# Logits of the first 128 rows: three products of rounded high and low parts in place of one product of whole fp32 values

## The chip, the cores and the metric

The kernel runs on one core of a Trainium2 chip. The time is device microseconds of that core, the median of several executions; the profile is one further execution. Engines: TensorE (PE for matmuls, PEld for its weight loads), VectorE (DVE), ScalarE (ACT), GpSimd (POOL) and SyncE (SP, which starts the large DMAs).

## The reference

Two layers over 256 tokens of width 1024, fp32 throughout. In each layer the normalised input goes through one input projection, whose columns serve two groups of heads: group A, sparse attention with 8 heads, whose keys are chosen by an indexer, and group B, differential attention with 4 pairs of maps, that is 8 maps too.

```python
for i in range(DEPTH):
    h = _rmsnorm(x, pre_norm_g[i])
    z = h @ w_in[i]
    qa, ka, va, qi, ki, wi, ga, qb, kb, vb, gb = _split_in(z)
    # rotary embedding on q and k of both groups
    oa = _dsa_attention(qa, ka, va, qi, ki, wi, top_k)   # logits = q k^T / 8, masked, softmax, times v
    ob = _diff_attention(qb, kb, vb, lam, lam_init, subln_g[i])
    y = jnp.concatenate([oa * jax.nn.silu(ga), ob * jax.nn.silu(gb)], axis=-1) @ w_out[i]
    x = x + _rmsnorm(y, post_norm_g[i])
    gate = jax.nn.sigmoid(x @ w_ple_gate[i])
    e = (p[i] @ w_ple_proj[i]) * gate
    x = x + _rmsnorm(e, ple_norm_g[i])
```

The attention is causal by chunks of 64 tokens. So rows 0 to 127 (block b = 0) need the keys 0 to 127 alone, and rows 128 to 255 (b = 1) need all 256.

## The kernel before

**Projections.** Each weight matrix is cut into units of 2 x 128 rows by 512 columns. ScalarE rounds a unit to fp32r (`w_hi`, line 637), VectorE subtracts that from the original (`w_lo`, line 835), and TensorE forms each product from three matmuls: high by high, high by low, low by high (lines 1233 to 1235). The activations are split in the same way. One step `mm` is a unit on one block of rows: 2 x 3 = 6 matmuls of 512 columns.

**Order.** `layer_steps` writes one list of steps for a layer, and every engine walks this same list and picks out its own part of each step. The projection chunks KB, VB, QA, KA, VA, GB, GA have 8 `mm` steps each, numbered 0, 1, 2, ... through all of them. `PLACE` says behind which of these numbers an attention step stands: `T` (transposes of q or k), `S` (logits), `E` (exponentials), `R` (reciprocals and mixing), `PT` (transposes of probabilities), `PV` (product with v). Within one number a `T` comes before an `S`, and both before an `E` and the `topk` rounds. The work of an engine runs strictly in this order, and semaphores tie the engines together.

**Queries and keys.** A step `T` transposes 128 tokens of a chunk with four PE transposes into the one PSUM bank `tr`. The next user of `tr` on PE, another `T` or a `PT`, waits until `tr` has been read (`wait_tr`, semaphore `tr_out`, line 1122). Who reads it depends on the block and chunk:

- queries, b = 0: ScalarE copies them whole, fp32, into `qT[g]` (line 714), and that frees `tr`;
- queries, b = 1: ScalarE writes the rounded `q_hi` (line 716), then VectorE `q_lo` (line 930), and that frees `tr`;
- keys, both blocks: ScalarE writes `k_hi` (line 720), then VectorE `k_lo` (line 934), and that frees `tr`. For b = 0 ScalarE first makes a whole copy `kT` (line 719).

**Logits.** `S` 0 and `S` 3 are the logits of b = 0 for groups B and A; `S` 1, 2, 4 and 5 are those of b = 1. Eight maps lie as four pairs: the even map of a pair on partitions 0 to 63, the odd one on 64 to 127, with 64 values per head. For b = 0 each map is one fp32 matmul of 128 queries by 128 keys from `qT` and `kT` (line 1161); for b = 1 it is three fp32r matmuls of 128 queries by 256 keys (lines 1163 and 1164). All are issued at line 1166. VectorE then adds the mask and takes the maximum (line 986), ScalarE the exponential (line 732).

`S` of b = 0 waits on `qk_hi_done`, that is on ScalarE's `k_hi` of the same keys; `S` of b = 1 waits on `tr_out` of its keys, that is on VectorE's `k_lo`. `kT` serves a second time, as the place of the last transposed probabilities. `p_hi` and `p_lo` hold the split per-layer embedding; they are read at a layer's first four `mm` steps and written again towards the end of the layer.

Of the kernel before, what the change touches and what calls it, by code (L numbers as in the profile page):

```python
# [22 lines left out]
P = 128  # L23
NB = SEQ // P
KT = D_MODEL // P
HEAD = 64
# [32 lines left out]
for _i, _u in enumerate(UNITS):  # L59
# [17 lines left out]
    QB=[5, 3],  # L77
    KB=[9, 12],
    QA=[25, 29],
    KA=[32, 37],  # L80
    S=[12, 15, 18, 34, 42, 43],
    E=[13, 16, 24, 36, 42, 43],
    R=[16, 16, 19, 19, 24, 24, 40, 43, 44, 44, 44, 45],
    PT=[19, 23, 26, 40, 41, 45, 46, 50, 51],
# [132 lines left out]
def build(nc, x, p, pre_norm_g, w_in, w_out, post_norm_g, lambda_q1, lambda_k1, lambda_q2, lambda_k2, subln_g,  # L217
# [6 lines left out]
    with ctx:  # L224
# [16 lines left out]
        p_hi = sb("p_hi", [P, NB, D_PLE // P, P], f32r)  # L241
# [11 lines left out]
        q_hi = sb("q_hi", [P, 4, P], f32r)  # L253
        q_lo = sb("q_lo", [P, 4, P], f32r)

        y_mix = [[qT[g][:, :, b * P:(b + 1) * P] for b in range(NB)] for g in range(2)]
        e_g = [qT[b][:, :, :].rearrange("p j t -> p (j t)") for b in range(NB)]
        probs = sb("probs", [P, 4, N])
# [120 lines left out]
        tr_steps = [s for s in layer_steps(0) if s[0] in ("TI", "T", "PT")]  # L379
        TRN = len(tr_steps)  # L380

        QK_WHOLE = [("QB", 0), ("QA", 0)]
        QK_SPLIT = [s[1:] for s in tr_steps if s[0] == "T" and s[1:] not in QK_WHOLE]

        def tr_index(L, s):

            return L * TRN + tr_steps.index(s) + 1
# [206 lines left out]
        def _(act):  # L594
            def copy(dst, src, scale=1.0):
                return nc.scalar.activation(dst, src, ACT.Copy, scale=scale)  # L596
# [27 lines left out]
            for pos, (L, s) in enumerate(STEPS):  # L624
# [83 lines left out]
                elif kind == "T":  # L708
                    chunk, b = s[1:]
                    act.wait_ge(tr_done, tr_index(L, s))  # L710
                    g, src = int(chunk[1] == "A"), tr[:, :].rearrange("p (j t) -> p j t", j=4)

                    if chunk[0] == "Q" and b == 0:
                        copy(qT[g][:, :, 0:P], src, HEAD ** -0.5).then_inc(tr_out, 1)
                    elif chunk[0] == "Q":
                        copy(q_hi[:, :, :], src, HEAD ** -0.5).then_inc(qk_hi_done, 1)
                    else:
                        if b == 0:
                            copy(kT[:, :, :], src)
                        copy(k_hi[:, :, b * P:(b + 1) * P], src).then_inc(qk_hi_done, 1)  # L720
                elif kind == "D":
                    for i in range(4):
# [74 lines left out]
        def _(dve):  # L797
# [31 lines left out]
            for pos, (L, s) in enumerate(STEPS):  # L829
# [89 lines left out]
                elif kind == "ylo":  # L919
# [1 line left out]
                    dve.wait_ge(at_hi, L * 12 + t8_index("y", b, 0) + 1)  # L921
                    nc.vector.tensor_tensor(act_lo[:, b, 0:4, :], y_mix[1][b], act_hi[:, b, 0:4, :].bitcast(fp32),
                                            ALU.subtract).then_inc(at_lo, 1)
                elif kind == "T" and s[1:] not in QK_WHOLE:

                    chunk, b = s[1:]
                    src = tr[:, :].rearrange("p (j t) -> p j t", j=4)
                    dve.wait_ge(qk_hi_done, L * 6 + QK_SPLIT.index(s[1:]) + 1)
                    if chunk[0] == "Q":
                        ins = nc.vector.scalar_tensor_tensor(q_lo[:, :, :], src, HEAD ** -0.5,  # L930
                                                             q_hi[:, :, :].bitcast(fp32), ALU.mult,
                                                             ALU.subtract)
                    else:
                        ins = nc.vector.tensor_tensor(k_lo[:, :, b * P:(b + 1) * P], src,  # L934
                                                      k_hi[:, :, b * P:(b + 1) * P].bitcast(fp32), ALU.subtract)
# [156 lines left out]
        def _(pe):  # L1092
# [60 lines left out]
            def logits(L, n, g, b, keys):  # L1153

                for j in range(N // keys):
                    for part in range(1 if b == 0 else 3):
                        for odd in range(2):
                            m = s_task(2 * n + odd)[2][j]
                            rows = slice(odd * HEAD, (odd + 1) * HEAD)
                            if b == 0:  # L1160
                                q, k = qT[g][rows, m // 2, 0:P], kT[rows, m // 2, :]
                            else:
                                q = (q_lo if part == 2 else q_hi)[rows, m // 2, :]
                                k = (k_lo if part == 1 else k_hi)[rows, m // 2, :]
                            end = part == (0 if b == 0 else 2)
                            ins = nc.tensor.matmul(s_bank(2 * n + odd)[:, j * keys:(j + 1) * keys], q, k,  # L1166
                                                   start=(part == 0), stop=end)
                            if end and j == N // keys - 1:
                                ins.then_inc(s_done, 1)
# [16 lines left out]
            for pos, (L, s) in enumerate(STEPS):  # L1186
# [147 lines left out]
                elif kind == "D":  # L1334

                    pe.wait_ge(tr_out, tr_index(L, ("TI", 1)))
                    pe.wait_ge(at_lo, L * 12 + 4)
                    for b in range(NB):
                        keys = (b + 1) * P
                        for j in range(2):  # L1340
                            for odd in range(2):
                                rows = slice(odd * HEAD, (odd + 1) * HEAD)
                                ins = nc.tensor.matmul(dots_of(b, odd)[:, j * keys:(j + 1) * keys],
                                                       idxT[rows, j, b * P:(b + 1) * P], idxT[rows, 2, 0:keys],
                                                       start=True, stop=True)
                                if j == 1:
                                    ins.then_inc(dots_done, 1)
                elif kind == "S" and s[1] not in S_WITH.values():
                    g, b, _, keys = s_task(2 * s[1])
                    keys_from = ("KB" if g == 0 else "KA", b)  # L1350
                    if b == 0:
                        pe.wait_ge(qk_hi_done, L * 6 + QK_SPLIT.index(keys_from) + 1)
                    else:
                        pe.wait_ge(tr_out, tr_index(L, ("T",) + keys_from))
                    if s[1] == 0:
                        pe.wait_ge(relu_done, L * 4 + 4)
                    else:
                        pe.wait_ge(max_done, L * 12 + {1: 2, 3: 4, 4: 8}[s[1]])
                    logits(L, s[1], g, b, keys)
                    if s[1] == 1:  # L1360
                        pe.wait_ge(z_out, L * 8 + 2)
                        logits(L, 2, g, b, keys)
                    elif s[1] == 4:
                        pe.wait_ge(max_done, L * 12 + 6)
                        logits(L, 5, g, b, keys)
                elif kind == "PT":
                    n = s[1]
                    g, b, tiles = pt_task(n)
                    wait_tr(L, s)
                    if g == 0:  # L1370
                        pe.wait_ge(mix_done, L * 3 + n + 1)
                    else:
                        pe.wait_ge(exp_done, L * 12 + tiles[1][2] + 1)
                    for j, (h, kt, si, col) in enumerate(tiles):
                        last = nc.tensor.transpose(tr[:, j * P:(j + 1) * P], probs[:, si % 4, col:col + P],  # L1375
                                                   ident[:, :])
                    last.then_inc(tr_done, 1)
                elif kind == "PV":
                    m = s[1]
                    g, b, _ = pt_task(PV_TASKS[m][0])  # L1380
                    pe.wait_ge(v_out, L * 4 + 2 * g + b + 1)
                    if m == 0:
                        pe.wait_ge(p_lo_done, L + 1)
                    for gi, (_, _, members) in enumerate(PV_GROUP):
                        if gi and m == members[0]:
                            pe.wait_ge(pv_out, L * 4 + gi)
                    pe.wait_ge(tr_out, tr_index(L, ("PT", PV_TASKS[m][-1])))
                    for n, j, (h, kt, si, col) in [(n, j, tile) for n in PV_TASKS[m]
                                                   for j, tile in enumerate(pt_task(n)[2])]:
                        if g == 0:  # L1390
                            last = nc.tensor.matmul(pv[:, h * P:(h + 1) * P], pt_slot(n)[:, j, :],  # L1391
                                                    v_all[:, kt, 0, h * P:(h + 1) * P], start=(kt == 0),
                                                    stop=(kt == b))
                        else:
                            rows = slice(h % 2 * HEAD, (h % 2 + 1) * HEAD)
                            last = nc.tensor.matmul(pv[rows, h // 2 * P:(h // 2 + 1) * P],  # L1396
                                                    v_all[:, kt, 1, h * HEAD:(h + 1) * HEAD], pt_slot(n)[:, j, :],
                                                    start=(kt == 0), stop=(kt == b), skip_group_check=True)
                    last.then_inc(pv_done, 1)
# [30 lines left out]
```

## Time and profile before

| | us |
|---|---|
| median of 3 executions | 359.07 (358.68 to 359.42) |
| the profiled execution, its own time | 359.26 |
| its span, first to last instruction | 357.5 |
| PE busy | 350.0 |
| PEld busy | 291.9 |
| DVE busy | 264.5 |
| ACT busy | 228.6 |
| POOL busy | 67.2 |

The mean granted clock of TensorE is 0.997 of full speed. In the views, "idle before" is the time that an engine stood still ahead of an instruction, and the arrow names what ended it. Where like instructions follow each other, a row gives the start of the first, the time from there to the end of the last, and their number. An fp32 matmul appears as two MATMUL records, an fp32r matmul as one (the page prints f32 for both), as the counts show: 8 fp32 matmuls in an `S` of b = 0 are 16 records.

### The profile page before, as it was taken

What the parts mean: (1) busy time and instruction counts of PE and PEld (TensorE: products, weight loads), DVE (VectorE), ACT (ScalarE), POOL (GpSimd) and SP (SyncE); (2) the same over time, 40 slices, a digit from 0 to 9 for tenths busy, and PEclk for the clock granted to TensorE, in tenths of its full rate; (3) what the DMA queues carried; (4) which work ended last, traced back from release to release, by engine and by line L of the source; (5) the groups of instructions that cost most, each with busy time, mean ns of one, the idle gap of its engine ahead of it and who ended that gap; (6) DMA issues with size and microseconds to landing.
All of it is one profiled execution on the core that took longest, in us unless ns stands there. A gap on an engine that the chain in (4) does not pass through costs nothing.

```text
span 357.5 us, 5709 instructions
## 1 busy us (share of the span) xinstructions
PE 350.0 (98%) x1927; PEld 291.9 (82%) x1927; DVE 264.5 (74%) x562; ACT 228.6 (64%) x459; POOL 67.2 (19%) x121
## 2 busy tenths in 40 slices
PE   8999999999999999999999999999999999999992
PEld 7887888888888888888888888788888888888882
DVE  3886979988946766786797487988895668678543
ACT  4897557777678945555757665778658686365221
POOL 1076261142200000013106433014220000000000
PEclk9999999999999999999999999999999999999998
DMA  7996488762754454647575927556355446550011
GB/s 287 381 336 216 130 193 200 257 177 68 224 169 131 129 195 149 210 158 154 179 231 158 353 82 207 147 129 178 107 168 155 151 141 213 175 169 11 0 50 69
DMA packets 31820, 61.12 MB, mean 171 GB/s; under 512 B 2376, under 2 KB 4432, under 8 KB 31792
## 3 DMA queue, kind: packets, MB, share of 16 engines
q1 hardware_dynamic: 30656, 57.48, 50.5%
q0 software_dynamic: 1120, 3.28, 4.8%
q8 instruction: 16, 0.26, 0.3%
q14 instruction: 12, 0.10, 0.1%
q10 hardware_dynamic: 16, 0.00, 0.0%
HBM read 59.71 MB, written 1.05 MB: 170 GB/s over the span
## 4 chain that ended last, share of the span: by engine, by line
PE 96%; issue 2%; DVE 1%; ACT 0%; POOLq 0%; DVEq 0%; POOL 0%
PE proj L1233 26%; PE proj L1235 25%; PE proj L1234 25%; PE sc L1314 3%; PE tr L1375 2%; PE sc L1166 2%; PE tr L1332 2%; PE pv L1396 2%; PE pv L1391 1%; PE proj L1177 1%; PE proj L1150 1%; PE proj L1166 1%; PE proj L1246 1%; PE proj L1139 1%; PE sc L1184 1%
## 5 line engine op out<-in xcount | busy, mean ns | idle before, releaser
L1233 PE MATMUL proj<-w_hi,act_hi 128*128 128x512 f32 (+1 forms) x392 | 157.4, 402 | 0.0
L1235 PE MATMUL proj<-w_hi,act_lo 128*128 128x512 f32 (+1 forms) x392 | 152.2, 388 | 0.0
L1234 PE MATMUL proj<-w_lo,act_hi 128*128 128x512 f32 (+1 forms) x392 | 151.6, 387 | 0.0
L835 DVE TENSOR_TENSOR w_lo<-raw,w_hi 128x1024 fp32r<-128x1024 f32 (+1 forms) x102 | 121.6, 1210 | 11.1 <-ACT w_hi L596 10.5
L596 ACT ACTIVATE w_hi<-raw 128x1024 fp32r<-128x1024 f32 (+2 forms) x103 | 102.5, 1022 | 2.4 <-PE proj L1235 1.8
L1235 PEld LDWEIGHTS proj<-w_hi,act_lo 128*128 128x128 f32 x392 | 73.5, 188 | 15.5
L1233 PEld LDWEIGHTS proj<-w_hi,act_hi 128*128 128x128 f32 x392 | 73.7, 188 | 14.6 <-issue 1.0
L1234 PEld LDWEIGHTS proj<-w_lo,act_hi 128*128 128x128 f32 x392 | 73.8, 188 | 12.8
L537 POOL TENSOR_TENSOR rstd<-var,minus_half 128x1 f32<-128x1 f32 x12 | 7.6, 640 | 191.6 <-DVE var L823 162.7
L732 ACT ACTIVATE probs<-probs,neg_max 128x128 f32<-128x128 f32 (+1 forms) x64 | 28.2, 444 | 6.0 <-DVE neg_max L986 6.0
L527 POOL TENSOR_TENSOR v_all<-work,rot_tab 128x128 f32<-128x128 f32 x16 | 10.6, 664 | 77.6 <-ACT work L596 77.5
L596 ACT ACTIVATE act_hi<-sc 128x512 fp32r<-128x512 f32 x20 | 11.3, 598 | 17.6 <-PE sc L1314 16.0
L596 ACT ACTIVATE pT<-tr 128x512 f32<-128x512 f32 (+1 forms) x20 | 11.4, 572 | 10.2 <-PE tr L1375 6.9
L915 DVE TENSOR_TENSOR act_lo<-sc,act_hi 128x512 fp32r<-128x512 f32 x16 | 10.4, 684 | 5.9 <-ACT act_hi L596 5.9
L934 DVE TENSOR_TENSOR k_lo<-tr,k_hi 128x512 fp32r<-128x512 f32 x8 | 5.5, 688 | 10.5 <-ACT k_hi L596 10.5
L732 ACT ACTIVATION_READ_ACCUMULATOR probs<-probs,neg_max 128x1 f32 x64 | 12.1, 189 | 0.0
L961 DVE MAX8 top<-score 128x8 f32<-128x128 f32 (+1 forms) x32 | 11.5, 358 | 0.6
L1375 PEld LDWEIGHTS tr<-ident,probs 128*128 128x128 f32 x72 | 8.8, 140 | 2.7 <-ACT pT L596 0.7
L962 DVE MATCH_REPLACE8 score<-top,score 128x128 f32<-128x128 f32 (+1 forms) x32 | 11.0, 343 | 0.0
L1375 PE MATMUL tr<-ident,probs 128*128 128x128 f32 x72 | 10.9, 273 | 0.0
L1051 DVE TENSOR_TENSOR work<-work,emb 128x512 f32<-128x512 f32 x7 | 4.8, 687 | 7.2 <-ACT work L768 7.2
L528 POOL TENSOR_TENSOR v_all<-work,rot_tab 128x64 f32<-128x64 f32 x16 | 10.1, 632 | 0.0
(209 smaller groups left out, 441.1 us busy)
## 6 DMA issues: line engine op xcount, KB each, us to landing
raw<-in_w_in_dram SPq DMA_DIRECT2D x59, 512.0 KB, 4.2
raw<-in_w_out_dram SPq DMA_DIRECT2D x16, 512.0 KB, 3.4
raw<-in_w_ple_gate_dram SPq DMA_DIRECT2D x16, 512.0 KB, 3.7
raw<-in_w_in_dram SPq DMA_DIRECT2D x7, 324.0 KB, 5.0
raw<-in_w_ple_proj_dram SPq DMA_DIRECT2D x4, 512.0 KB, 4.2
resid<-in_x_dram SPq DMA_DIRECT2D x2, 512.0 KB, 6.2
probs<-in_w_in_dram SPq DMA_DIRECT2D x2, 512.0 KB, 9.2
g_ple<-in_ple_norm_g_dram POOLq DMA_DIRECT2D x2, 512.0 KB, 7.3
```

The source lines that it names most:

```text
L527: nc.gpsimd.tensor_tensor(rot_a[:, 0:heads, :], view[:, :, 0:ROT], table(cos2, slice(0, ROT)), ALU.mult)
L596: return nc.scalar.activation(dst, src, ACT.Copy, scale=scale)
L732: last = nc.scalar.activation(probs[:, i % 4, j * keys:(j + 1) * keys], probs[:, i % 4, j * keys:(j + 1) * keys], ACT.Exp, bias=neg_max[:, ...
L835: nc.vector.tensor_tensor(w_lo[:, g % SLOTS, 0:nk * cols], landing(g, nk * cols), w_hi[:, g % SLOTS, 0:nk * cols].bitcast(fp32), ALU.subtr ...
L961: link(nc.vector.max(top8[:, :], score[b][:, :]))
L962: link(nc.vector.match_replace(score[b][:, :], top8[:, :], score[b][:, :], TAKEN))
L1166: ins = nc.tensor.matmul(s_bank(2 * n + odd)[:, j * keys:(j + 1) * keys], q, k, start=(part == 0), stop=end)
L1233: nc.tensor.matmul(ps, src_hi[:, b, k0 + k, :], hi, start=(first_u and k == 0), stop=False)
L1234: nc.tensor.matmul(ps, src_hi[:, b, k0 + k, :], lo, start=False, stop=False)
L1235: last = nc.tensor.matmul(ps, src_lo[:, b, k0 + k, :], hi, start=False, stop=last_k)
L1314: last = nc.tensor.transpose(sc[i % 2][:, j * P:(j + 1) * P], tile, ident[:, :])
L1375: last = nc.tensor.transpose(tr[:, j * P:(j + 1) * P], probs[:, si % 4, col:col + P], ident[:, :])
```

## The change

The logits of b = 0 are formed as those of b = 1: from `q_hi`, `q_lo`, `k_hi`, `k_lo` in three fp32r matmuls, on the 128 keys of the block. The high and low parts of its queries lie in the memory of `p_hi` and `p_lo`. VectorE gets two more steps per layer (`q0_lo` for QB and QA), ScalarE loses two (`kT`), and its copy of the queries is now the rounding one. `S` of b = 0 waits on `tr_out`. `S` 3 stands one `mm` step later, behind number 35.

```diff
-    S=[12, 15, 18, 34, 42, 43],
+    S=[12, 15, 18, 35, 42, 43],
...
+        q0_hi, q0_lo = (tile[:, :, :, :].rearrange("p b k t -> p (b k) t") for tile in (p_hi, p_lo))
...
-        QK_WHOLE = [("QB", 0), ("QA", 0)]
-        QK_SPLIT = [s[1:] for s in tr_steps if s[0] == "T" and s[1:] not in QK_WHOLE]
+        QK_SPLIT = [s[1:] for s in tr_steps if s[0] == "T"]
...  (ScalarE, step T)
-                    if chunk[0] == "Q" and b == 0:
-                        copy(qT[g][:, :, 0:P], src, HEAD ** -0.5).then_inc(tr_out, 1)
-                    elif chunk[0] == "Q":
-                        copy(q_hi[:, :, :], src, HEAD ** -0.5).then_inc(qk_hi_done, 1)
+                    if chunk[0] == "Q":
+                        copy((q_hi if b else q0_hi)[:, :, :], src, HEAD ** -0.5).then_inc(qk_hi_done, 1)
                     else:
-                        if b == 0:
-                            copy(kT[:, :, :], src)
                         copy(k_hi[:, :, b * P:(b + 1) * P], src).then_inc(qk_hi_done, 1)
...  (VectorE, step T)
-                elif kind == "T" and s[1:] not in QK_WHOLE:
+                elif kind == "T":
...
-                    dve.wait_ge(qk_hi_done, L * 6 + QK_SPLIT.index(s[1:]) + 1)
+                    dve.wait_ge(qk_hi_done, L * 8 + QK_SPLIT.index(s[1:]) + 1)
                     if chunk[0] == "Q":
-                        ins = nc.vector.scalar_tensor_tensor(q_lo[:, :, :], src, HEAD ** -0.5,
-                                                             q_hi[:, :, :].bitcast(fp32), ALU.mult,
-                                                             ALU.subtract)
+                        hi, lo = (q_hi, q_lo) if b else (q0_hi, q0_lo)
+                        ins = nc.vector.scalar_tensor_tensor(lo[:, :, :], src, HEAD ** -0.5,
+                                                             hi[:, :, :].bitcast(fp32), ALU.mult, ALU.subtract)
...  (TensorE, logits)
-                    for part in range(1 if b == 0 else 3):
+                    for part in range(3):
                         for odd in range(2):
...
-                            if b == 0:
-                                q, k = qT[g][rows, m // 2, 0:P], kT[rows, m // 2, :]
-                            else:
-                                q = (q_lo if part == 2 else q_hi)[rows, m // 2, :]
-                                k = (k_lo if part == 1 else k_hi)[rows, m // 2, :]
-                            end = part == (0 if b == 0 else 2)
+                            hi, lo = (q_hi, q_lo) if b else (q0_hi, q0_lo)
+                            q = (lo if part == 2 else hi)[rows, m // 2, :]
+                            k = (k_lo if part == 1 else k_hi)[rows, m // 2, 0:keys]
+                            end = part == 2
...  (TensorE, step S)
-                    if b == 0:
-                        pe.wait_ge(qk_hi_done, L * 6 + QK_SPLIT.index(keys_from) + 1)
-                    else:
-                        pe.wait_ge(tr_out, tr_index(L, ("T",) + keys_from))
+                    pe.wait_ge(tr_out, tr_index(L, ("T",) + keys_from))
```

## Rows read from the trace of the kernel before

**Rows 1.** The page: span, and the chain that ended last, by engine.

```profile
span 357.5 us, 5709 instructions
...
PE 96%; issue 2%; DVE 1%; ACT 0%; POOLq 0%; DVEq 0%; POOL 0%
```

**Rows 2.** Waits of PE over the whole span: line, waited for, total us, times, longest.

```profile
PE sc L1184 <- DVE score L800: 1.1, 1, 1.1
```

**Rows 3.** Line 1166, all its matmuls: count, duration ns min/median/max, first and last start.

```profile
L1166 PEld LDWEIGHTS sc<-kT,qT_b x32: 182/188/188, 54.5 to 227.3; 64*128 64x128 f32 x32
L1166 PE MATMUL sc<-kT,qT_b x32: 272/272/373, 54.5 to 227.4; 64*128 64x128 f32 x32
L1166 PE MATMUL sc<-k_lo,q_hi x16: 275/278/278, 60.1 to 279.4; 64*128 64x256 f32 x16
L1166 PEld LDWEIGHTS proj<-k_hi,q_hi x16: 185/186/186, 60.6 to 279.8; 64*128 64x128 f32 x16
```

**Rows 4.** Timeline of PE around S 0 of layer 0: start us, us, what, count.

```profile
54.46 1.16 PE L1166 MATMUL sc<-kT,qT_b 64*128 64x128 f32 x16
55.55 0.50 PE L1233 MATMUL proj<-w_hi,act_hi 128*128 128x512 f32 x1
55.88 0.40 PE L1234 MATMUL proj<-w_lo,act_hi 128*128 128x512 f32 x1
```

**Rows 5.** Timeline of PE around S 1 and S 2 of layer 0.

```profile
59.87 0.38 PE L1166 MATMUL sc<-k_hi,q_hi 64*128 64x256 f32 x2
60.10 0.28 PE L1166 MATMUL sc<-k_lo,q_hi 64*128 64x256 f32 x2
60.21 0.28 PE L1166 MATMUL sc<-k_hi,q_lo 64*128 64x256 f32 x2
...
61.28 0.28 PE L1166 MATMUL proj<-k_hi,q_lo 64*128 64x256 f32 x2
61.49 0.50 PE L1233 MATMUL proj<-w_hi,act_hi 128*128 128x512 f32 x1
```

**Rows 6.** Weight loads of 64 columns (line 1396) and of transposes (line 1375), whole span.

```profile
L1396 PEld LDWEIGHTS pv<-pT,v_all x80: 132/137/137, 108.4 to 298.9; 128*64 128x64 f32 x80
L1375 PEld LDWEIGHTS tr<-ident,probs x72: 138/140/144, 66.8 to 295.6; 128*128 128x128 f32 x72
```

**Rows 7.** Groups of PE by form: 512 and 256 columns, all rows of the array.

```profile
L1234 PE MATMUL proj<-w_lo,act_hi 128*128 128x512 f32 x376 | 146.7, 390 | 0.0
L1222 PE MATMUL proj<-w_lo,act_hi 128*128 128x256 f32 x8 | 2.3, 283 | 0.0
```

**Rows 8.** Timeline from T of QA, b = 0, to PT 2, layer 0.

```profile
77.99 0.60 PE L1332 MATMUL tr<-ident,work 128*128 128x128 f32 x4
78.62 0.60 ACT L596 ACTIVATE qT_a<-tr 128x512 f32<-128x512 f32 x1 [0.46 <-PE tr L1332]
78.63 0.42 DVE L961 MAX8 top<-score 128x8 f32<-128x256 f32 x1
...
79.81 0.60 PE L1375 MATMUL tr<-ident,probs 128*128 128x128 f32 x4
```

**Rows 9.** The same place in layer 1.

```profile
250.64 0.60 ACT L596 ACTIVATE qT_a<-tr 128x512 f32<-128x512 f32 x1 [0.53 <-PE tr L1332]
...
251.84 0.60 PE L1375 MATMUL tr<-ident,probs 128*128 128x128 f32 x4
```

**Rows 10.** Two hand-overs, layer 0: ScalarE to VectorE (KA, b = 1), VectorE to PE (QB, b = 1).

```profile
100.54 0.57 ACT L596 ACTIVATE k_hi<-tr 128x512 fp32r<-128x512 f32 x1
101.15 0.69 DVE L934 TENSOR_TENSOR k_lo<-tr,k_hi 128x512 fp32r<-128x512 f32 x1 [3.28 <-ACT k_hi L596]
...
42.57 0.69 DVE L930 SCALAR_TENSOR_TENSOR q_lo<-tr,q_hi 128x512 fp32r<-128x512 f32 x1
...
43.44 0.60 PE L1332 MATMUL tr<-ident,work 128*128 128x128 f32 x4
```

**Rows 11.** Timeline of DVE from the topk rounds to S 3, layer 0.

```profile
85.70 0.17 DVE L1017 TENSOR_SCALAR var_h<-ssq_h 128x4 f32<-128x4 f32 x1 [1.06 <-ACT qT_b L749]
...
93.23 0.68 DVE L934 TENSOR_TENSOR k_lo<-tr,k_hi 128x512 fp32r<-128x512 f32 x1
```

**Rows 12.** Timeline of PE: before S 3, S 3 of layer 0, and PT 3 behind it.

```profile
92.36 0.39 PE L1233 MATMUL proj<-w_hi,act_hi 128*128 128x512 f32 x1
92.58 0.39 PE L1234 MATMUL proj<-w_lo,act_hi 128*128 128x512 f32 x1
92.81 0.39 PE L1235 MATMUL proj<-w_hi,act_lo 128*128 128x512 f32 x1
93.13 1.16 PE L1166 MATMUL sc<-kT,qT_a 64*128 64x128 f32 x16
...
103.01 0.60 PE L1375 MATMUL tr<-ident,probs 128*128 128x128 f32 x4
```

**Rows 13.** ScalarE behind S 3 of layer 0: first and last exponential.

```profile
96.50 0.39 ACT L732 ACTIVATE probs<-probs,neg_max 128x128 f32<-128x128 f32 x1
...
99.50 0.19 ACT L732 ACTIVATION_READ_ACCUMULATOR probs<-probs,neg_max 128x1 f32 x1
```

**Rows 14.** Around T of QB and of KB, b = 0, layer 0.

```profile
45.52 0.28 DVE L961 MAX8 top<-score 128x8 f32<-128x128 f32 x1
...
49.36 0.60 PE L1332 MATMUL tr<-ident,work 128*128 128x128 f32 x4
```

More of the change, by code:

```diff
@@ L710, in _ @@
                     act.wait_ge(tr_done, tr_index(L, s))
-                    g, src = int(chunk[1] == "A"), tr[:, :].rearrange("p (j t) -> p j t", j=4)
-                    if chunk[0] == "Q" and b == 0:
-                        copy(qT[g][:, :, 0:P], src, HEAD ** -0.5).then_inc(tr_out, 1)
-                    elif chunk[0] == "Q":
-                        copy(q_hi[:, :, :], src, HEAD ** -0.5).then_inc(qk_hi_done, 1)
-                    else:
-                        if b == 0:
-                            copy(kT[:, :, :], src)
+                    src = tr[:, :].rearrange("p (j t) -> p j t", j=4)
+                    if chunk[0] == "Q":
+                        copy((q_hi if b else q0_hi)[:, :, :], src, HEAD ** -0.5).then_inc(qk_hi_done, 1)
+                    else:
                         copy(k_hi[:, :, b * P:(b + 1) * P], src).then_inc(qk_hi_done, 1)
```

## The prediction

> **What bounds the kernel now.** I read the page first, for the chain that ended last: 96% of the span is PE [rows 1]. The table of waits then says how closely PE is packed: in 357.5 us it waits once, 1.1 us at the very start [rows 2]. So each nanosecond added to PE's own stream, or to a wait that comes to stand before it, lengthens the kernel by as much, and relief of ScalarE or VectorE is worth nothing unless PE waits for them. The timelines around `T`, `S` and `PT` then give the two prices that are needed: what a block of logits takes of PE, and how near the next user of `tr` stands behind its last reader.
>
> **Part 1: the matmuls of S 0 and S 3.** There are four such blocks, two per layer. Now a block is 8 fp32 matmuls, 16 records, in pairs on the two halves of the array: 8 pairs of records. From its first matmul to the next projection matmul it takes 55.55 - 54.46 = 1.09 us [rows 4]. Its last record starts 1.16 - 0.27 = 0.89 us after the first. The b = 1 block shows that the first pair is dearer (60.10 - 59.87 = 0.23 us), so the other six gaps are (0.89 - 0.23) / 6 = 0.11 us each, and 0.20 us pass from the last pair to the projection.
>
> After the change there are 8 x 3 = 24 records, 12 pairs, each of 128 columns in fp32r. The trace has no fp32r matmul narrower than 256 columns, so the gap between its pairs has to be bounded. Two things take part in it. Streaming: an fp32r matmul lasts 390 ns at 512 columns and 283 at 256 [rows 7], so 0.42 ns a column, the full clock, one pass; 128 columns are 53 ns of streaming. The fp32 record of 128 columns lasts 272 ns, as long as 256 columns of fp32r (278) [rows 3], so it is two passes, and an fp32 matmul four. Loading: each record loads 128 columns of weights, which shows as 188 ns, and 64 columns as 137 ns [rows 3, 6]. The difference is 51 ns for 64 columns, 0.8 ns a column, so some 102 ns for 128. In the b = 1 block both the streaming (107) and the loading (102) fit into its gap of (61.28 - 60.10) / 10 = 0.118 us [rows 5]. They are covered by each other, and a narrower matmul shortens one of them alone.
>
> - Lower end: streaming alone sets the gap, 53 ns and the 11 ns that the b = 1 gap has over its 107, so 0.065 us. Block: 0.23 + 10 x 0.065 + 0.15 (the tail is a pass shorter) = 1.03 us, a gain of 0.06, in four blocks 0.2 us.
> - Loading sets it: 0.11 to 0.118 us. Block: 0.23 + 10 x 0.11 (or 0.118) + 0.15 to 0.20 = 1.48 to 1.61 us. This is 0.39 to 0.52 more.
> - Upper end: a narrow fp32r matmul is not one pass but the four of fp32, 213 ns. Block: 0.23 + 10 x 0.22 + 0.30 = 2.73 us, 1.64 more, in four blocks 6.6 us.
>
> I take the second, 0.45 us a block and **1.8 us in all**: the b = 1 block is the nearest row, with the same number of pairs (12), the same loads and the same order of parts, and it takes 61.49 - 59.87 = 1.62 us [rows 5]. One thing speaks against loads at 0.8 ns a column: the load ahead of a transpose has 128 columns too and shows 140 ns [rows 6], so not every fp32 load is slow. But the loads for logits show 182 to 188 ns before and for both kinds [rows 3].
>
> A load's price is also stated by the Trainium skill, "TensorE: Matmul & The Clock Gate", section "LDWEIGHTS (loading the stationary operand)": columns over 1.2, so 107 ns for 128; by it the gap could not be under 107 ns. The difference of the two load rows [rows 3, 6] agrees with it (0.8 ns a column), and the row of the transposes does not.
>
> **Part 2: T of QA, b = 0, and PT 2 behind it.** The transposes into `tr` stand at number 25, `PT` 2 at 26, one `mm` step later. Now ScalarE's copy ends at 78.62 + 0.60 = 79.22 and PE's transposes of `PT` 2 start at 79.81, in stream [rows 8]. After the change `tr` is free only when VectorE has written `q0_lo`. Hand-over from ScalarE 101.15 - (100.54 + 0.57) = 0.04 us, 0.69 us for the subtraction, then from its end to PE's first transpose 43.44 - (42.57 + 0.69) = 0.18 us [rows 10] (there PE was hardly held up, so this is rather an upper value). VectorE is free in time: the instruction before ends as ScalarE starts (78.63) [rows 8]. Sum: 79.22 + 0.04 + 0.69 + 0.18 = 80.13, 0.32 us after 79.81. In layer 1: 250.64 + 0.60 + 0.91 = 252.15 against 251.84, 0.31 us [rows 9]. Queued behind the waiting PT 2 is all of PE's stream, so this is **0.6 us in all**. Bounds: 0, if the hand-overs shrink or if the ordinary gap between stream and transposes takes them in; 1.2, if VectorE comes a subtraction late.
>
> **Part 3: what is hidden.** T of QB, b = 0: `q0_lo` can start when the two `w_lo` before it end, at 45.52, and is done at 46.2, while T of KB, the next user of `tr`, starts at 49.36 [rows 14]; 3 us of cover. VectorE waits at number 25 for ScalarE and then works 0.69 us, so what follows it there starts 79.95 - 78.63 = 1.3 us later. Of this PE's own 0.3 us is no loss, and 1.06 us go into the idle time ahead of line 1017 [rows 11]. So `k_lo` of KA, b = 0, is in place with PE again: it ends at 93.91 [rows 11], and S 3, which now waits for it, starts at 93.13 plus one `mm` step (6 matmuls at (92.81 - 92.36) / 2 = 0.225, so 1.35), 94.48 [rows 12]; 0.6 us to spare. At the old place, 34, it would have waited 0.8 us. If VectorE is over 0.6 us late, S 3 stalls by the rest; that is kept in the range with up to 0.7 us a layer.
>
> S 3 being 1.35 us later and 0.45 longer, its exponentials: VectorE starts at 94.82 + 1.45 = 96.3, four maps of 0.21 us are ready at 97.2, the eight exponentials take 99.69 - 96.50 = 3.2 us [rows 13] and end at 100.4. PT 3, which needs them, starts at 103.01 [rows 12] and moves later too. The two whole copies (0.60 us of ScalarE each) fall away where ScalarE had nothing behind it that PE waits for: I count nothing for them. The memory of `p_hi` and `p_lo` is read by the layer's first steps, long done at T of QB: no wait.
>
> **Sum.** 359.26 + 1.8 + 0.6 = 361.7 against the profiled execution, which is 0.19 over the median: **361.5 us**, 0.7% slower. Its own range is 360.4 to 362.8.
>
> **The rivals.**
>
> - **Not slower: the passes set the price.** For it: an fp32 matmul has four passes and the three fp32r ones have three, so streaming falls by a quarter, and loads of 140 ns exist [rows 6]. It decides from a gap of 0.072 us per pair on (0.23 + 10 x 0.072 + 0.15 = 1.09, even). At its end, 53 ns a gap and no surplus, a block takes 0.91 us, four gain 0.7; with part 2's 0.6 the time is 359.0. Against it: the load rows of these very matmuls. The skill's "FP8 and Floating Point Precision", section "TensorE Precision Notes", has fp32 as four passes, which speaks for this rival as a count of passes; the rows [rows 3] show the same four.
> - **In between: loads overlap more than I hold.** A gap of 0.081 us would give a block of 1.19, +0.1, and 360.1 us. The skill's clock-gate page, section "Back-to-back issue gap", states about 81 ns for a stream of load and 128-column matmul; no row here has such a stream in fp32r. The same rows speak for and against as above.
> - **Slower by far: narrow fp32r is no single pass.** If it ran as fp32 does, the upper end above, 6.6 + 0.6 makes 366.3 us. For it: nothing in the trace, only that nothing at 128 columns excludes it. Against: the duration is linear from 512 to 256 columns [rows 7].
> - **VectorE as the new bound.** It gets 4 x 0.69 us; if it comes late to `k_lo` or the masks, PE waits at S 3: 361.5 + 2 x 0.7 = 362.9. Against it: the idle time of 1.06 us just ahead.
>
> **How the numbers follow.** Forecast 0.54, VectorE late 0.06, passes alone 0.08, in between 0.12, narrow matmuls at four passes 0.20. A difference of 0.2%, 0.7 us, is about the least that a measurement can tell from none, so "same" is 358.4 to 359.8. The forecast, the late VectorE and the four passes are slower, and so are two thirds of the case in between: 0.80 + 0.08 = 0.88, less 0.04 for what I have not seen: 0.84. Of the passes alone a third would come out faster: with the unseen 0.04. Same: 0.12. The range has to reach to the four passes, since that case alone has 0.20, and down to the case in between: 359.5 to 366.6.
>
> **What would show it.** In the new trace: 24 records at line 1166 for each b = 0 block, 1.48 to 1.61 us from its first matmul to the next line 1233, a duration near 225 ns per matmul (272 less one pass) at loads of 188. A duration of 380 would be the four passes; gaps of 0.065 between pairs the passes alone. PE idle of 0.3 us ahead of PT 2, ended by VectorE's `q0_lo`, twice. No PE wait at S 3 nor at T of KB. Wrong would be a block under 1.1 us, or a stall at S 3, or a difference that lies neither in the blocks nor at PT 2.

## The result, and the profile after

The changed kernel takes 364.44 us (median of 5, 363.82 to 365.29) against 359.22 us: 1.48% slower, ratio 1.0148 with a 95% interval of 1.0133 to 1.0163, or 5.2 us. The prediction was 361.5 us: slower, as forecast, but by 5.2 us instead of 2.3.

Its profiled execution has a span of 362.6 us, against 357.5. The table of waits of PE shows what is new: line, waited for, total us, times, longest.

```profile
PE tr L1367 <- DVE p_lo L928: 2.7, 2, 1.4
PE sc L1179 <- DVE score L797: 1.1, 1, 1.1
PE proj L1241 <- DVE w_hi L877: 0.2, 1, 0.2
```

The first row was not there in [rows 2]: twice, once a layer, PE stands still ahead of the transposes of `PT` 2 (line 1367) until VectorE has written `q0_lo` (it lies in `p_lo`). The timeline of PE and ScalarE at this place in layer 0, which answers to [rows 8], and VectorE's queue beside it:

```profile
78.74 0.60 PE L1327 MATMUL tr<-ident,work 128*128 128x128 f32 x4
79.38 0.60 ACT L597 ACTIVATE p_hi<-tr 128x512 fp32r<-128x512 f32 x1 [0.44 <-PE tr L1327]
79.41 0.42 DVE L958 MAX8 top<-score 128x8 f32<-128x256 f32 x1
79.87 0.09 DVE L959 MATCH_VALUE_LOAD score<-top,score 128x8 f32 x1
79.94 0.41 DVE L959 MATCH_REPLACE8 score<-top,score 128x256 f32<-128x256 f32 x1
80.39 0.43 DVE L958 MAX8 top<-score 128x8 f32<-128x256 f32 x1
80.85 0.09 DVE L959 MATCH_VALUE_LOAD score<-top,score 128x8 f32 x1
80.93 0.41 DVE L959 MATCH_REPLACE8 score<-top,score 128x256 f32<-128x256 f32 x1
81.37 0.69 DVE L928 SCALAR_TENSOR_TENSOR p_lo<-tr,p_hi 128x512 fp32r<-128x512 f32 x1
81.98 0.42 DVE L958 MAX8 top<-score 128x8 f32<-128x256 f32 x1
...
82.11 0.66 PE L1367 MATMUL tr<-ident,probs 128*128 128x128 f32 x4 [1.38 <-DVE p_lo L928]
...
85.37 1.05 PE L1383 MATMUL pv<-v_all,pT 128*128 128x128 f32 x8
```

ScalarE is done at 79.98, but VectorE is in the middle of two rounds of topk, and `q0_lo` starts at 81.37, 1.4 us late. The idle time of 1.38 us is counted from the end of the last matmul's record (80.34 + 0.40). The delay of the start is larger: in stream `PT` 2 would start one matmul, 0.23 us, behind 80.34, so at 80.57, and it starts at 82.11, 1.54 us later. From T of QA to the matmuls of `PV` 2 (line 1383) it is 85.37 - 78.74 = 6.63 us. Before, the same stretch was

```profile
83.00 1.05 PE L1391 MATMUL pv<-v_all,pT 128*128 128x128 f32 x8
```

83.00 - 77.99 = 5.01 us. The loss is 1.62 us. In layer 1 it is (259.73 - 253.19) - (255.02 - 250.00) = 1.52 us.

The blocks of logits cost a little less than forecast (0.45 us more for each). `S` 0 of layer 0, PE's timeline, beside [rows 4]:

```profile
54.85 0.33 PE L1161 MATMUL sc<-k_hi,p_hi 64*128 64x128 f32 x2
55.01 0.28 PE L1161 MATMUL sc<-k_lo,p_hi 64*128 64x128 f32 x2
...
56.13 0.28 PE L1161 MATMUL sc<-k_hi,p_lo 64*128 64x128 f32 x2
56.34 0.51 PE L1228 MATMUL proj<-w_hi,act_hi 128*128 128x512 f32 x1
```

56.34 - 54.85 = 1.49 us against 1.09, so 0.40 more, with a gap between pairs of (56.13 - 55.01) / 10 = 0.112 us. Four blocks: 1.6 us.

Set side by side at the same steps, the profiled executions part by 0.4 us before the first logits, by 4 x 0.39 at the blocks and by 1.62 + 1.52 at `PT` 2: 0.4 + 1.6 + 3.1 = 5.1 us, the whole of 362.6 - 357.5. The 0.4 us arises at 5 to 8 us from the start, at the first projection matmuls, where no instruction differs. It is the spread between executions: T of KB, b = 1, of layer 0 starts at 54.32 us here, and at 53.60 us in experiment 7, whose kernel is the same up to that place, against 53.93 before. Over the nine experiments whose traces can be compared it starts between 53.6 and 55.8 us.

### The profile page after: what moved, and what is told of

Its sections match the earlier page's. It is cut to its first block, busy times and chain, and to the rows that moved or that the text cites. A ratio compares the mean times of both kernels' runs of the same rounds, so it can differ in the third digit from the quotient of the medians.

```text
span 362.6 us, 5775 instructions
## 1 busy us (share of the span) xinstructions
PE 352.3 (97%) x1959; PEld 293.7 (81%) x1959; DVE 266.8 (74%) x566; ACT 226.8 (63%) x455; POOL 67.3 (19%) x121
## 4 chain that ended last, share of the span: by engine, by line
PE 90%; DVE 3%; issue 2%; ACT 2%; DMA 1%; POOLq 0%; DVEq 0%; POOL 0%; SPq 0%
PE proj L1228 24%; PE proj L1230 24%; PE proj L1229 24%; PE sc L1161 3%; PE sc L1309 2%; PE tr L1367 2%; PE tr L1327 2%; PE pv L1388 2%; PE proj L1147 1%; PE proj L1172 1%; DMA raw<-in_w_ple_proj_dram 1%; ACT probs L729 1%; PE pv L1383 1%; PE proj L1161 1%; PE proj L1241 1%
## 5 line engine op out<-in xcount | busy, mean ns | idle before, releaser
L533 POOL TENSOR_TENSOR work<-v_all 128x128 f32<-128x128 f32 x16 | 10.5, 655 | 1.3
```

The source lines that it names most:

```text
L533: nc.gpsimd.tensor_tensor(view[:, :, 0:ROT], rot_a[:, 0:heads, :], rot_b[:, 0:heads, :], ALU.add).then_inc(done, 1)
```

## The experiments

**1. The wait alone.** The kernel before, with its logits, but VectorE frees the bank. Here and below the edits are shortened.

```diff
-  copy(qT[g][:, :, 0:P], src, HEAD ** -0.5).then_inc(tr_out, 1)
+  copy(qT[g][:, :, 0:P], src, HEAD ** -0.5).then_inc(qk_hi_done, 1)
...  (VectorE, T of a Q chunk, b == 0)
+  scalar_tensor_tensor(q0_lo, src, HEAD ** -0.5, qT[g][:, :, 0:P], mult, subtract).then_inc(tr_out, 1)
```

> The kernel before, its logits untouched (whole fp32 values, kT kept, S 3 at 34), but VectorE also computes a low part of the queries of rows 0 to 127, which nobody reads, and it is this that frees the bank. Queue theory: PT 2 waits for it 1.5 to 1.6 us in each layer, 359.2 + 3.1 = 362.3 us. Rival as in the prediction (VectorE free in time): 0.6 us, 359.8. Rival, the stall is lost in slack further on: 359.2.

Measured: 362.30 us, ratio 1.0085 (1.0070 to 1.0099), so +3.0 us. The waits of PE:

```profile
PE tr L1379 <- DVE p_lo L930: 2.7, 2, 1.4
PE sc L1188 <- DVE score L800: 1.0, 1, 1.0
```

The row is the same as in the changed kernel, with nothing of the logits touched. In its trace the stall has the size of the changed kernel's too (1.38 us of idle in layer 0, and 84.50 - 77.87 = 6.63 us from T of QA to `PV` 2). My own term of 0.6 us (359.8) is out, and so is slack further on.

**2. The two topk rounds behind.** The changed kernel with one list edited.

```diff
-  topk=[[0, 0, 2, 6, 6, 7, 10, 11], [12, 24, 24, 25, 26, 26, 27, 31]],
+  topk=[[0, 0, 2, 6, 6, 7, 10, 11], [12, 25, 25, 25, 26, 26, 27, 31]],
```

> The changed kernel with VectorE's two topk rounds of number 24 moved to 25, so that q0_lo of QA stands ahead of them in its queue. Queue theory: in the changed kernel q0_lo waits 1.96 us behind these two rounds (79.41 to 81.37), and PT 2 waits for it; with the rounds behind it q0_lo starts as ScalarE ends, and PT 2 stalls 0.3 us a layer instead of 1.55. Time 364.4 - 2 x 1.25 = 361.9 us, idle of PE ahead of PT 2 0.3 us or less. Rival, the hand-over through VectorE is slow in itself or the bank is held by something else: PT 2 stalls 1.4 us as before, 364.4 us.

Measured: 361.44 us, ratio 1.0066 (1.0049 to 1.0084). PE, ScalarE and VectorE at that place in layer 0:

```profile
78.61 0.60 PE L1327 MATMUL tr<-ident,work 128*128 128x128 f32 x4
...
79.24 0.60 ACT L597 ACTIVATE p_hi<-tr 128x512 fp32r<-128x512 f32 x1 [0.44 <-PE tr L1327]
...
79.88 0.69 DVE L928 SCALAR_TENSOR_TENSOR p_lo<-tr,p_hi 128x512 fp32r<-128x512 f32 x1 [0.52 <-ACT p_hi L597]
...
83.88 1.05 PE L1383 MATMUL pv<-v_all,pT 128*128 128x128 f32 x8
```

VectorE now waits for ScalarE and starts 0.04 us after it. The stretch to `PV` 2 is 83.88 - 78.61 = 5.27 us, 0.26 over the kernel before, and 0.24 in layer 1. The late subtraction was therefore a matter of the order in VectorE's queue alone; the hand-over itself costs the 0.3 us a layer that the prediction gave it. The time is 3.0 us under the changed kernel's, of which the trace shows (1.62 - 0.26) + (1.52 - 0.24) = 2.6 at this place; the rest is of the size of the spread at the start.

**3. The blocks alone.** 24 matmuls per block, no `q0_lo`.

```diff
-  hi, lo = (q_hi, q_lo) if b else (q0_hi, q0_lo)
+  hi, lo = (q_hi, q_lo) if b else (q0_hi, q0_hi)
...  (ScalarE, T of a Q chunk, b == 0; VectorE skips the step)
+  copy(q0_hi[:, :, :], src, HEAD ** -0.5).then_inc(tr_out, 1)
```

> Leaves out the low part of the queries of rows 0 to 127: the third product takes the high part again, VectorE has no q0_lo, and ScalarE's rounding copy frees the bank, as before the change. All 24 matmuls of each of the four blocks stay. Theory: blocks are 1.49 us instead of 1.09, four of them, nothing else: 359.2 + 1.6 = 360.8 us, no PE wait at PT 2. Rival, the blocks cost only through what follows them (exponentials, later S 3): PE waits appear elsewhere and the time is above 361.5. Rival, the 0.4 us by which the changed kernel was late already at 8 us of its trace belongs to the change: 361.2 us.

Measured: 360.98 us, ratio 1.0054 (1.0037 to 1.0072), +1.7 us, and no wait of PE at `PT` 2 or `S`. Experiments 1 and 3 together make 3.04 + 1.72 = 4.8 us of the 5.2; the 0.4 us left is within their intervals, of about 0.5 us each. Of the two rivals, the one of waits elsewhere is out. The one of 361.2 us lies inside the interval and is not told from the theory by the time; it falls by the comparison of starts above.

**4. Two products.** As 3, and the third product left out.

```diff
-  for part in range(3):
+  for part in range(3 if b else 2):
...
-  end = part == 2
+  end = part == (2 if b else 1)
```

> Leaves out the third product (low part of the queries) for rows 0 to 127: 16 fp32r matmuls per block, 8 pairs, bank freed by ScalarE as before the change. If each pair costs 0.111 us, by its loads or by a floor, a block is 1.05 us, as the 16 records of the fp32 form (1.09), and the time is that of before, 359.2 (359.0 to 359.4). If a block of fp32r has a cost of its own that is not per pair, the time is over 359.8.

Measured: 359.26 us, ratio 0.9997 (0.9982 to 1.0012). `S` 0 of layer 0, its first pair and the projection behind it:

```profile
54.72 0.33 PE L1164 MATMUL sc<-k_hi,p_hi 64*128 64x128 f32 x2
...
55.76 0.51 PE L1231 MATMUL proj<-w_hi,act_hi 128*128 128x512 f32 x1
```

The block takes 1.04 us, against 1.09 for the fp32 form. Each map has two records, as in the fp32 form, and the time is the same: the price goes by the number of records. Whether it is their loads or a floor per record is for the next two to tell. The two whole copies of ScalarE are gone here too and bring nothing that the time shows.

**5. Loads of 64 columns, and 6. streams of 64 columns.** Both on the kernel of 3.

```diff
(experiment 5: half the queries)
-  q = (lo if part == 2 else hi)[rows, m // 2, :]
+  q = (lo if part == 2 else hi)[rows, m // 2, 0:P if b else HEAD]
(experiment 6: half the keys)
-  k = (k_lo if part == 1 else k_hi)[rows, m // 2, 0:keys]
+  k = (k_lo if part == 1 else k_hi)[rows, m // 2, 0:keys if b else HEAD]
...  (in both, the part of the PSUM bank that is written is halved to match)
```

> Like the kernel with the blocks alone (three products, no q0_lo), but for rows 0 to 127 only the first 64 queries are computed: each matmul loads 64 weight columns and streams 128 key columns. Load theory: the load falls to 51 ns of columns, the gap between pairs falls from 0.111 to about 0.065 us (streaming 53 plus 11), a block to 1.0 us, the time to 358.8. Rival, a fp32r matmul of 128 columns streams no faster than one of 256 (its records last 275 ns, as those of 256 columns): the gap stays 0.11 us, 360.8.

> Like the kernel with the blocks alone, but for rows 0 to 127 each matmul streams only 64 key columns under 128 weight columns (the other keys are left out). Load theory: the gap between pairs stays 0.107 to 0.111 us, since the load is the same, and the record still lasts about 275 ns. Rival, streaming sets the gap at two cycles a column or so: 0.055 to 0.065 us.

Measured for 5: 358.73 us, ratio 0.9978 (0.9960 to 0.9995). For 6, a single execution: 360.65 us; its weight lies in the trace. Records of line 1164 (duration ns min/median/max) and PE's timeline of `S` 0, first with loads of 64:

```profile
L1164 PEld LDWEIGHTS sc<-k_lo,p_hi x32: 131/132/135, 56.4 to 268.3; 64*64 64x64 f32 x32
L1164 PE MATMUL sc<-k_lo,p_hi x32: 217/220/226, 56.4 to 268.3; 64*64 64x128 f32 x32
...
56.30 0.28 PE L1164 MATMUL sc<-k_hi,p_hi 64*64 64x128 f32 x2
56.41 0.23 PE L1164 MATMUL sc<-k_lo,p_hi 64*64 64x128 f32 x2
...
57.01 0.23 PE L1164 MATMUL sc<-k_hi,p_hi 64*64 64x128 f32 x2
57.17 0.50 PE L1231 MATMUL proj<-w_hi,act_hi 128*128 128x512 f32 x1
```

and with streams of 64:

```profile
L1164 PEld LDWEIGHTS sc<-k_lo,p_hi x32: 186/188/188, 54.5 to 268.7; 64*128 64x128 f32 x32
L1164 PE MATMUL sc<-k_lo,p_hi x32: 272/273/274, 54.5 to 268.7; 64*128 64x64 f32 x32
...
54.40 0.30 PE L1164 MATMUL sc<-k_hi,p_hi 64*128 64x64 f32 x2
54.53 0.28 PE L1164 MATMUL sc<-k_lo,p_hi 64*128 64x64 f32 x2
...
55.65 0.28 PE L1164 MATMUL sc<-k_hi,p_hi 64*128 64x64 f32 x2
55.86 0.50 PE L1231 MATMUL proj<-w_hi,act_hi 128*128 128x512 f32 x1
```

Half the load columns (and with them half the rows of the result): the gap falls from 0.112 to (57.01 - 56.41) / 10 = 0.060 us, the block from 1.49 to 0.87. Half the stream columns: the gap is still (55.65 - 54.53) / 10 = 0.112, the block 1.46. So at 128 weight columns the load sets the gap, and neither the stream nor a floor per record does: the floor is at most 0.060 us. At 64 weight columns the load and a stream of 128 columns come to about the same by the forecast's prices (51 and 53 ns), so the 0.060 does not say which of them holds there.

**7. S 3 back at 34.** `S=[12, 15, 18, 34, 42, 43]` in the changed kernel.

> The changed kernel with S 3 back at its place of before, number 34. In the trace of the changed kernel k_lo of KA ends at 96.28 and S 3 starts at 96.85; a step earlier it would start at 95.49. Theory: PE then waits for k_lo some 0.85 us in each layer, 364.4 + 1.7 = 366.1 us. Rival, the later place buys nothing, since VectorE's exponentials and masks follow earlier and give it back: 364.4.

Measured: 365.75 us, ratio 1.0181 (1.0165 to 1.0196). Its waits of PE have a new row (expected: 0.85 us a layer):

```profile
PE tr L1367 <- DVE p_lo L928: 2.6, 2, 1.4
PE sc L1161 <- DVE k_lo L931: 1.5, 2, 0.8
```

Each wait is 0.77 us, and the 1.3 us over the changed kernel agree with two of them; the expected 366.1 us were 0.35 too many. The later place of `S` 3 is worth that much once the block needs `k_lo`.

**8. PT 2 one step later too.** On the kernel of 2: `PT=[19, 23, 27, ...]`, `PV=[20, 25, 29, ...]`. The expectation of its first timing:

> The changed kernel with the two topk rounds at 25 and also PT 2 at 27 and PV 2 at 29, one mm step later each. Theory: PT 2 no longer waits for q0_lo at all, 364.4 - 3.1 = 361.3 us, of which 1.6 are the blocks. Rival, the later PV 2 holds up the mean of squares and T of QA, b = 1, behind it on ScalarE and VectorE: a new wait, 361.9 or more.

and of a second run of the same kernel, whose trace is the one that is read here:

> The same kernel as the one with PT 2 at 27, for a second profile. The first look gave 362.7 us, above the 361.4 us of the kernel with only the topk rounds moved. Theory now: a new wait has come in behind the later PT 2 or PV 2, of about 0.7 us a layer; the table of PE's waits or the gap ahead of GB, T of QA b = 1 or VectorE's line 1023 shows it. Rival: no new wait, the time was disturbed, and it comes out at 361.0 to 361.4.

Measured: 362.74 and 362.65 us, ratios 1.0090 (1.0060 to 1.0121) and 1.0108 (1.0078 to 1.0138). The stall at `PT` 2 is gone, and others have come. PE's waits, and in layer 0 VectorE from `PV` 2 to `k_lo` with what waits for it on PE:

```profile
PE sc L1161 <- DVE k_lo L931: 1.1, 2, 0.6
...
87.69 0.17 DVE L1014 TENSOR_SCALAR var_h<-ssq_h 128x4 f32<-128x4 f32 x1 [1.24 <-ACT qT_b L746]
...
89.89 0.68 DVE L928 SCALAR_TENSOR_TENSOR q_lo<-tr,q_hi 128x512 fp32r<-128x512 f32 x1
...
90.62 0.42 PEld L1327 LDWEIGHTS tr<-ident,work 128*128 128x128 f32 x4 [0.44 <-DVE q_lo L928]
...
95.17 0.68 DVE L931 TENSOR_TENSOR k_lo<-tr,k_hi 128x512 fp32r<-128x512 f32 x1
...
95.91 0.33 PE L1161 MATMUL sc<-k_hi,p_hi 64*128 64x128 f32 x2 [0.50 <-DVE k_lo L931]
```

In experiment 2 the three VectorE steps start at 86.58, 88.78 and 94.10. With `PV` 2 later, ScalarE's squares of its result end later, VectorE stands idle for 1.24 us until it can take the variance from them (line 1014), and all that is behind it in its queue comes 1.1 us later: `q_lo`, with T of KA behind it, and `k_lo`, for which `S` 3 waits 0.5 us a layer. ScalarE is not what holds up `q_lo`: its `q_hi` starts only 0.16 us later than in experiment 2 (87.47 against 87.31). The slack that `PT` 2 gained was that of the next chain. My first theory (361.3) fell; the rival held.

**9. Two products everywhere.** The third product is left out for rows 128 to 255 too, and `q_lo` with it.

```diff
-  for part in range(3 if b else 2):
+  for part in range(2):
```

> Leaves out the third product (low part of the queries) in all logits, for rows 128 to 255 too, with q_lo dropped. For rows 0 to 127 it is 16 records a block, even with the kernel before; for the others each of the four blocks (S 1 with S 2, S 4 with S 5, two layers) falls from 12 pairs to 8 at 0.118 us. Per-pair theory: 359.3 - 4 x 4 x 0.118 = 357.4 us. Rival, these blocks end in a wait on VectorE's maxima, which takes the gain: 359.3.

Measured: 357.58 us, ratio 0.9956 (0.9943 to 0.9970). That is 1.8 us less than before, of the 4 x 4 x 0.118 = 1.9 expected. It is the one version that computes all logits and beats both kernels, at less precision: the low part of the queries is missing in it.

## Why the prediction was wrong

**What bounds the kernel: right.** Every price found stood in PE's stream or ahead of it and came out in the time to within 0.3 us (experiments 1, 3, 5, 9). The relief of ScalarE brought nothing that shows (experiment 4).

**Part 1, the matmuls: right in cause, a little high in size.** Forecast 0.45 us a block and 1.8 in all; the trace has 0.40 and 1.6, the blocks alone 1.7. The gap came out as forecast (0.112 against 0.11 to 0.118); the first pair, put at 0.23 us, took 55.01 - 54.85 = 0.16. The load sets the gap, as experiments 5 and 6 show. The rival of the passes alone (a gap of 0.053 to 0.065) and the four-pass rival (0.22) are both out.

The gap of the rival in between, 0.081 us, is out as well. The Trainium skill, "TensorE: Matmul & The Clock Gate", section "Back-to-back issue gap", states about 81 ns per matmul for a stream of loads and 128-column matmuls; here the matmuls of one half of the array, each with its load, follow each other at 112 ns. The Trainium skill's rule on loads in "LDWEIGHTS (loading the stationary operand)" of the same page, a time in ns of the columns over 1.2, makes 107 ns at 128 columns and 53 ns at 64 as estimates; the gaps here are 112 and 60 ns, 5 to 7 above them.

**Part 2, PT 2: this step failed.** The sentence is "VectorE is free in time: the instruction before ends as ScalarE starts (78.63)". The row at 78.63 [rows 8] is a MAX8, and I took it for the first of what follows the new subtraction. It is what precedes it. `PLACE` has the topk rounds of rows 128 to 255 at 12, 24, 24, 25: two rounds belong to number 24, and T of QA to 25. They fill VectorE from 79.41 to 81.37, and the subtraction is in the queue behind them. Within a number T comes first; I applied that order to rounds of the number before. The term was 0.6 us and is 3.1.

The trace of the kernel before holds the right sum. The first row of number 25 in it, the one ahead of which the subtraction stands, is this:

```profile
80.59 0.43 DVE L961 MAX8 top<-score 128x8 f32<-128x256 f32 x1
```

80.59 + 0.69 + 0.18 = 81.46 is 1.65 us after 79.81. In layer 1 that row is at 252.54, and 253.41 is 1.57 us after 251.84: 3.2 us in all, against 3.1 measured. The upper bound of the term was too low by its own words as well: one subtraction late in each layer makes 2 x (0.31 + 0.69) = 2.0 us and not 1.2. Experiment 2, where the two rounds do stand behind, gives the forecast's own world: 361.4 us against 361.5, and 0.26 us a layer against 0.32.

**Part 3: right in its outcome, with other terms.** There was no wait at T of KB or at `S` 3, and at the old place of `S` 3 the measured wait is 0.77 us a layer (forecast 0.8). The forecast let VectorE's queue behind the subtraction come 1.3 us later. The MAX8 behind it moved by 81.98 - 80.59 = 1.39 us, but 0.78 of that is there before the subtraction already (79.41 against 78.63, the same instruction), since PE was late; the subtraction adds the other 0.6. PE, with its stall, was 85.37 - 83.00 = 2.37 us late at `PV` 2. Ahead of the variance VectorE waits for the squares of what `PV` 2 gives, so its own lateness is taken up by that idle time, which is 2.05 us here, against 1.06 before [rows 11], since PE came later still:

```profile
88.07 0.17 DVE L1014 TENSOR_SCALAR var_h<-ssq_h 128x4 f32<-128x4 f32 x1 [2.05 <-ACT qT_b L746]
...
95.59 0.69 DVE L931 TENSOR_TENSOR k_lo<-tr,k_hi 128x512 fp32r<-128x512 f32 x1
...
96.85 0.33 PE L1161 MATMUL sc<-k_hi,p_hi 64*128 64x128 f32 x2
```

The variance is 88.07 - 85.70 = 2.37 us later than before, and `k_lo` by 2.36; `S` 3 starts 2.37 us behind the forecast's 94.48. So `k_lo` still ended 0.6 us ahead of it (96.28 against 96.85). In experiment 2, where PE is hardly held up, it is 0.6 us as well (94.78 against 95.38). One number of this part is off without consequence: VectorE's maxima of `S` 3 start at 94.96 in the trace of before and not at 94.82.

**Sum.** 1.8 + 0.6 against 1.6 + 3.1, and 0.4 us that no part of the change accounts for. The range held the time by luck: only because it reached to the four-pass rival, which is not what happened. "A difference that lies neither in the blocks nor at PT 2" did not come; one at PT 2 of five times the size did.

## What to carry to other kernels

When a step gives an engine a new instruction that another engine waits for, write down that engine's queue in front of it, by the program's order and not by the trace's times: a row that starts where the new instruction would start may well stand ahead of it. And a split into three narrow products trades four passes under two loads for three passes under three loads. At 128 stream columns a pair costs 0.11 us in either form, so three products lose to two records. At 256 columns a pair of fp32 records costs 0.217 us and one of fp32r 0.118 (next section); by these gaps three products (0.35 us) would win over two records (0.43), though no run here sets the two forms of the same logits side by side at that width. Count loads where the load is the longer of the two, and passes where the stream is. Slack taken for one wait (experiment 8) is to be looked for in the chain behind it first.

## What the runs showed of the hardware

- On logits with 64 rows in pairs, the gap between pairs is 0.112 us with 128 weight columns, for 128 stream columns and for 64 alike, 0.118 us for 256, and 0.060 us with 64 weight columns and 128 stream columns.
- A matmul's record is no measure of its stream: 128 columns of fp32r last 272 ns behind loads of 188 and 220 ns behind loads of 132, and 64 columns of stream still last 273. I had forecast 225 for the changed kernel, and had read two passes out of fp32's 272 at 128 columns, which shows nothing.
- That an fp32 record streams twice as long as an fp32r one is seen where the load does not cover it, at 256 columns, in the kernel before (the indexer's dots, fp32) beside [rows 3] and [rows 5]. The record lasts 376 ns against 278 at the same loads. The second row below has four pairs, the last of which starts 1.03 - 0.38 = 0.65 us after the first: a gap of 0.217 us against 0.118.

```profile
L1343 PE MATMUL sc<-pT x16: 376/376/378, 33.7 to 206.3; 64*128 64x256 f32 x16
...
33.68 1.03 PE L1343 MATMUL sc<-pT 64*128 64x256 f32 x8
```
